# Delta rule steps of a two-block transformer kernel: inverse as three factors, 16-blocks solved on VectorE, two parts of neighbouring steps interleaved

## The chip, the cores and the metric

The kernel runs on one core of a Trainium2 chip, all in 32-bit floats, with batch 1 and 256 tokens. The metric is the device time of one execution in microseconds (us), lower is better. The engines are named as in the profile: PE (TensorE), DVE (VectorE), ACT (ScalarE), POOL (GpSimd) and SP (SyncE, which issues most transfers).

## What is computed

The program computes two transformer blocks. The first has dilated attention, a convolution branch, attention to a memory, and a mixture of 32 experts. The second works on 256 latent tokens and 256 context tokens: a state-space mixer (SSD), a gated delta rule (GDN) with 8 heads of 128, both in two directions and with the context's final state as the latents' first one, then a feed-forward layer. The change is in the gated delta rule. The reference solves a unit lower triangular system per chunk and head:

```python
def gdn_chunk_scan(q, k, v, log_a, beta, s0):
    ...
    a_mat = jnp.einsum("bclhd,bcshd->bclsh", k, k) * beta[:, :, :, None] * masked_exp(diff, strict)
    lhs = jnp.moveaxis(a_mat, -1, 2) + jnp.eye(CHUNK, dtype=a_mat.dtype)
    rhs = jnp.concatenate([v * beta[..., None], k * (beta * jnp.exp(g))[..., None]], -1)
    sol = lax.linalg.triangular_solve(lhs, jnp.moveaxis(rhs, 3, 2), left_side=True,
                                      lower=True, unit_diagonal=True)
    ...
    def step(s, inp):
        u_c, w_c, qk_c, qg_c, kd_c, dec_c = inp
        v_new = u_c - jnp.einsum("bhlk,bhkv->bhlv", w_c, s)
        o = jnp.einsum("bhlk,bhkv->bhlv", qg_c, s) + jnp.einsum("bhls,bhsv->bhlv", qk_c, v_new)
        s = s * dec_c[..., None, None] + jnp.einsum("bhlk,bhlv->bhkv", kd_c, v_new)
        return s, o
```

## The kernel before

The kernel takes chunks of 128 tokens, so each direction has four steps: two over the context, two over the latents. The table `STEPS` puts them in the order m = 0 to 7, directions alternating, so that step m needs the state of step m - 2. Steps 0 to 3 (context) are woven between the phases of the 32 experts by `mixed_schedule`, which gives each phase a cost and spreads the context phases over the expert phases in proportion; all engines follow that one list. Steps 4 to 7 (latents, `LATENT`) follow the SSD stage, after the experts, with parts of the modulation rows (`mod_part`, `mod_sum`, of a weight tile `ad4` to `ad11`) put between their phases.

Weights stream from HBM through a ring of six slots of 1 MB. SP issues a transfer when the piece that held the slot has been used by PE (`wait_freed`). In the experts stage each half of gate and up and each down product takes two slots.

PE writes into six banks of PSUM in turn (`MAIN`): `open_tile` waits until the tile six places earlier has been drained by ACT or DVE. One tile holds four heads, so each quantity of a step has two tiles, h = 0 and 1. `("gKK", m, h)` is the tile of that name.

Within a step the functions `gdn_pe`, `gdn_act`, `gdn_dve` and `gdn_pool` walk the same phases. "rows" transposes the keys and makes the rows of summed log decays (a matmul of a broadcast column with a triangular mask); "gram" makes K K^T, which DVE multiplies with beta and decay into the strictly triangular matrix A. Its inverse is formed in whole: the blocks of 16 on the diagonal by a product of powers (P2, X2, X4, X8), and then three levels of merging (32, 64, 128), each with a transpose (XT), a product (T) and another (Y), masks by POOL between them. "w" and "v" then apply it to the scaled keys and values, and "S" makes output (go2) and new state (gS). No phase of step m + 1 begins before the last of step m.

The recorded durations of an f32 matmul stand in two rows of the trace, and those of a transpose in one.

## Time and profile before

| | |
|---|---|
| median of 3 runs | 1868.62 us (1863.86 to 1870.5) |
| the profiled execution | 1869.31 us |
| its span | 1867.6 us, granted clock 0.956 |
| PE busy | 1708.2 us (91%) |
| DVE, ACT, POOL busy | 684.6 (37%), 435.7 (23%), 213.2 us (11%) |
| HBM read | 369.98 MB, 199 GB/s over the span |
| experts stage | about 440 to 1040 us |
| second block up to the delta steps | 1040 to 1293 us |
| delta steps 4 to 7 | 1293 to 1531 us |
| projection, feed-forward | 1531 to 1868 us |

Busy is the time in which an engine executes something that counts; waits aren't in it. The span is that of the profiled execution on the chip, a little shorter than its time, which the clock of the runs measures. A stage's bound is read from its own window, not from the share over the whole span.

### The profile page before, as it was taken

How to read it: one execution, taken by the hardware profiler on the slowest of the kernel's cores; microseconds unless marked ns; L12 is line 12 of the kernel's file. 1: busy time of each engine (PE TensorE's matmuls, PEld its weight loads, DVE VectorE, ACT ScalarE, POOL GpSimd, SP SyncE). 2: the span in 40 equal slices, each digit the busy share in tenths (PEclk: the TensorE clock that was granted, in tenths of full speed). 3: DMA queues.
4: the chain of work that ended last, by engine and by line, in shares of the span. 5: the costliest groups of instructions: out<-in, count | busy, mean ns of one | idle time of the engine just before them, and what ended most of it. 6: DMA issues, size and time to landing. Idle time of an engine off the chain costs nothing.

```text
span 1867.6 us, 25449 instructions
## 1 busy us (share of the span) xinstructions
PE 1708.2 (91%) x10656; PEld 1209.9 (65%) x10656; DVE 684.6 (37%) x1404; ACT 435.7 (23%) x889; POOL 213.2 (11%) x190
## 2 busy tenths in 40 slices
PE   7999999999888879999999899899989989699996
PEld 3558555456666547767766588666978874488842
DVE  2107113335434353323233377665355450400003
ACT  1010454013111123323332231322333430000000
POOL 2000000020000012221212100011342320100000
PEclk9999999998988889999999899999999999799998
DMA  7444335723999888979989434224121222244340
GB/s 242 163 148 143 128 125 190 251 103 135 372 394 350 326 317 343 416 318 365 415 340 393 171 137 148 90 91 176 62 91 46 91 91 90 90 138 178 123 155 38
DMA packets 124295, 372.69 MB, mean 200 GB/s; under 512 B 10523, under 2 KB 26517, under 8 KB 107413
## 3 DMA queue, kind: packets, MB, share of 16 engines
q1 hardware_dynamic: 118245, 361.12, 51.6%
q0 software_dynamic: 1568, 8.39, 1.2%
q10 hardware_dynamic: 4368, 1.54, 0.4%
q8 instruction: 87, 1.43, 0.3%
q14 instruction: 27, 0.22, 0.0%
HBM read 369.98 MB, written 1.05 MB: 199 GB/s over the span
## 4 chain that ended last, share of the span: by engine, by line
PE 77%; DMA 13%; DVE 7%; ACT 1%; issue 1%; SPq 0%; DVEq 0%; ACTq 0%
PE psum L1976 49%; PE psum L571 10%; DMA ring<-in_w_down 4%; PE psum L1775 4%; DMA ring<-in_w_up 4%; DMA ring<-in_w_in 4%; PE psum L1970 3%; PE psum L1816 2%; PE psum L1759 2%; PE psum L1797 1%; PE psum L2093 1%; PE psum L768 1%; PE psum L2123 1%; PE psum L557 1%; DVE area L1180 1%
## 5 line engine op out<-in xcount | busy, mean ns | idle before, releaser
L1976 PE MATMUL psum<-area,ring 128*128 128x256 f32 x1984 | 457.7, 391 | 15.1 <-DMA ring<-in_w_in 14.1
L1976 PE MATMUL psum<-ring,area 128*128 128x512 f32 (+1 forms) x1040 | 452.5, 595 | 8.6 <-DMA ring<-in_w_proj_mem 2.4
L1976 PEld LDWEIGHTS psum<-area,ring 128*128 128x128 f32 x1984 | 386.1, 197 | 75.2 <-DMA ring<-in_w_in 18.1
L1976 PEld LDWEIGHTS psum<-ring,area 128*128 128x128 f32 x1040 | 198.9, 193 | 252.7 <-issue 251.7
L571 PEld LDWEIGHTS psum<-area 128*128 128x128 f32 x2304 | 269.7, 194 | 34.7 <-issue 19.1
L571 PE MATMUL psum<-area 128*128 128x128 f32 x2304 | 281.0, 280 | 10.6 <-DVE area L1180 10.4
L949 ACT ACTIVATE area<-psum 128x512 f32<-128x512 f32 x236 | 138.7, 597 | 243.7 <-PE psum L571 127.8
L2249 ACT ACTIVATE area<-psum 128x512 f32<-128x512 f32 x116 | 66.4, 599 | 460.9 <-PE psum L1976 362.2
L1970 PE MATMUL psum<-const,area 128*128 128x128 f32 x736 | 120.6, 294 | 52.0 <-DVE area L1490 14.8
L1970 PEld LDWEIGHTS psum<-const,area 128*128 128x128 f32 x736 | 90.5, 149 | 97.4 <-issue 23.0
L1775 PE MATMUL psum<-ring,area 128*32 128x256 f32 x2048 | 124.8, 388 | 12.5 <-DMA ring<-in_w_up 12.3
L1775 PEld LDWEIGHTS psum<-ring,area 128*32 128x32 f32 x2048 | 64.0, 111 | 59.3 <-issue 24.0
L1144 DVE SCALAR_TENSOR_TENSOR area<-area,cols 128x268 f32<-128x268 f32 (+1 forms) x186 | 91.6, 492 | 6.6
L1797 PE MATMUL psum<-ring,area 128*32 128x256 f32 x1024 | 68.2, 398 | 19.8 <-DMA ring<-in_w_down 19.4
L1535 POOL TENSOR_TENSOR area<-area,const 128x512 f32<-128x512 f32 x48 | 60.1, 1274 | 219.2 <-PE psum L571 219.2
L913 ACT COPY area<-psum 128x256 f32<-128x256 f32 x62 | 23.1, 373 | 210.6 <-PE psum L1976 210.6
L1142 DVE TENSOR_SCALAR area<-area,cols 128x268 f32<-128x268 f32 (+1 forms) x62 | 22.1, 356 | 120.3 <-ACT area L913 119.1
L1514 POOL TENSOR_TENSOR area<-area 128x1024 f32<-128x1024 f32 x4 | 10.8, 2728 | 461.9 <-DVE area L2371 461.9
L1797 PEld LDWEIGHTS psum<-ring,area 128*32 128x32 f32 x1024 | 31.0, 113 | 50.0 <-DMA ring<-in_w_down 22.0
L1501 DVE TENSOR_TENSOR area<-psum,area 128x512 f32<-128x512 f32 x11 | 7.6, 691 | 151.5 <-PE psum L1976 151.5
L1232 DVE TENSOR_TENSOR area<-area,psum 128x512 f32<-128x512 f32 x48 | 32.9, 687 | 67.2 <-PE psum L571 67.1
L1222 DVE TENSOR_TENSOR area<-psum,area 128x512 f32<-128x512 f32 x48 | 33.2, 691 | 60.7 <-PE psum L571 60.2
(304 smaller groups left out, 1346.5 us busy)
## 6 DMA issues: line engine op xcount, KB each, us to landing
ring<-in_w_gate SPq DMA_DIRECT2D x64, 1024.0 KB, 9.6
ring<-in_w_up SPq DMA_DIRECT2D x64, 1024.0 KB, 11.5
ring<-in_w_down SPq DMA_DIRECT2D x64, 1024.0 KB, 11.3
ring<-in_w_in SPq DMA_DIRECT2D x29, 2048.0 KB, 8.4
ring<-in_w_ada SPq DMA_DIRECT2D x12, 2048.0 KB, 8.1
ring<-in_w_in SPq DMA_DIRECT2D x13, 1024.0 KB, 7.5
ring<-in_w_out SPq DMA_DIRECT2D x6, 2048.0 KB, 8.5
ring<-in_w_ffn_gate SPq DMA_DIRECT2D x5, 2048.0 KB, 7.8
```

Source lines behind the costliest of these rows:

```text
L571: last = nc.tensor.matmul(dst[:, i * P:(i + 1) * P], lhs(i), rhs(i), start=True, stop=True)
L949: nc.scalar.activation(dst, src, ACT.Copy, scale=scale).then_inc(drain_of(key), 1)
L1144: link(v.scalar_tensor_tensor(dst, src, w, dst, ALU.mult, ALU.add))
L1222: v.tensor_tensor(bb[h][7], four(key), bb[h][7], ALU.add).then_inc(drain_of(key), 1)
L1535: g.tensor_tensor(b[6], b[3], by_row(LEVELS[lev]), ALU.mult).then_inc(s["level_ready"], 1)
L1759: last = nc.tensor.matmul(dst[:, j * P:(j + 1) * P], h2[:, t, k * P:(k + 1) * P], place[:, t, q * P:(q + 1) * P], start=t == 0, stop=t == ...
L1775: last = nc.tensor.matmul(wide.dst[CAP * j:CAP * (j + 1), 0:2 * P], hcT[:, q % 2, k, rows], both[:, :, k % 4, j * P:(j + 1) * P], start=k ...
L1797: last = nc.tensor.matmul(dst[CAP * g:CAP * (g + 1), 0:256], actT_e[:, e % 2, CAP * j:CAP * (j + 1)], w[:, j % 2, g * 256:(g + 1) * 256], ...
L1816: nc.tensor.matmul(dst, placeT[:, q, t * P:(t + 1) * P], y_quad[:, q % 2, half * WIDE:(half + 1) * WIDE], start=True, stop=True).then_inc( ...
L1970: last = nc.tensor.transpose(t[0:width, j * P:j * P + rows], src, ident[0:rows, 0:rows])
L1976: last = nc.tensor.matmul(dst, lhs(k), rhs(k), start=first and k == 0, stop=final and k == count - 1)
L2249: nc.scalar.activation(dst, src, func).then_inc(drain_of(key), 1)
```

## The change

The step no longer forms the inverse in whole. A is split into its diagonal blocks of 16 and the rest. The blocks' inverse X comes from a recurrence over 15 columns on DVE, for all 64 blocks and heads at once: A's blocks are gathered to rows of 16, spread with a unit pattern to 2048 columns, PE sums them over each block with the mask `blk16` in four matmuls of 512 columns (gRep), so that each partition has its block's whole 16x16 matrix; then come 15 pairs of a product and a subtraction, each waiting for the one before, and eight writes into XT. With M = A_off X and M2 = M M, the inverse is applied to the right-hand side as factors (M2 is used twice, in gT and gw, and again in gx, and M once, in gv) rather than formed. What it is applied to is U = v beta less the scaled K S (gK), so the keys need no inverse of their own. The rows of summed decays are made by transposing a broadcast column of `cum`; the SSD stage's rows too. POOL no longer masks levels.

`delta_phases` puts the part of step m + 1 that needs no state (rows, gram, rep) between the phases of step m (kS, M, u, M2, t, w, x, v, out); the costs of the schedule between the experts follow that. The modulation tiles, the q sums and the normalized y of the SSD have new places in it. Per step PE's products of all heads go down to 14 from 23 in the latents.

```diff
+def delta_phases(steps):
+
+    order = [(phase, steps[0]) for phase in ("rows", "gram", "rep")]
+    for m in steps:
+        for phase in ("kS", "M", "rows", "u", "M2", "gram", "t", "w", "rep", "x", "v", "out"):
+            if phase not in ("rows", "gram", "rep"):
+                order.append((phase, m))
+            elif m + 1 in steps:
+                order.append((phase, m + 1))
+    return order
...
+    delta = {"rows": 2.4, "gram": 2.0, "rep": 3.6, "kS": 1.9, "M": 3.8, "u": 1.9, "M2": 1.9, "t": 1.9, "w": 1.9, "x": 1.9,
+             "v": 1.9, "out": 1.9}
...
+        MOD_PHASES = ["gram 4", "rep 4", "kS 4", "v 4", "v 5", "v 6", "u 7", "w 7", "v 7"]
...
+                        transposes(("gR", m, h), [cum[side][:, d, t, 16 + head:17 + head].to_broadcast([P, P])
+                                                  for head in range(4 * h, 4 * h + 4)])
...
+                if phase == "rep":
+                    pe.wait_ge(s["spread_ready"], m + 1)
+                    columns = b["spread"].rearrange("p i h j -> p (i h j)")
+                    for q in range(4):
+                        nc.tensor.matmul(open_tile(("gRep", m, q)), blk16, columns[:, 512 * q:512 * q + 512],
+                                         start=True, stop=True).then_inc(filled, 1)
+                if phase == "kS" and ci:
+                    for h in range(2):
+                        wait_drained(pe, ("gS", m - 2, h))
+                        eight("gK", h, of("kT"), lambda head: state[:, head, :])
+                if phase == "M":
+                    pe.wait_ge(s["XT_ready"], m + 1)
+                    for h in range(2):
+                        pe.wait_ge(s["off_ready"], 2 * m + h + 1)
+                        eight("gM", h, of("XT"), of("A"))
+                        eight("gMT", h, of("A"), of("XT"))
...
+                if phase == "v":
+                    for h in range(2):
+                        wait_drained(pe, ("gx", m, h))
+                        eight("gv", h, of("MT"), of("U"))
...
+                    for q in range(4):
+                        part = slice(32 * q, 32 * q + 32)
+                        ins = v.tensor_copy(b["pairs"][part, :, :], b["A"][part, :, part])
...
+                if phase == "rep":
+                    rep, Y, tmp = b["rep"], b["Y"], b["step"]
+                    link(v.tensor_copy(Y, unit_16.unsqueeze(2).to_broadcast([P, 16, GDN_HEADS])))
+                    for q in range(4):
+                        wait_drained(eng, ("gRep", m, q))
+                    for j in (range(15), range(15, 0, -1))[d]:
+                        left = (slice(j + 1, 16), slice(0, j))[d]
+                        n = left.stop - left.start
+                        link(v.tensor_tensor(tmp[:, 0:n, :], rep[:, left, :, j], Y[:, j:j + 1, :].to_broadcast([P, n, GDN_HEADS]), ALU.mult))
+                        link(v.tensor_tensor(Y[:, left, :], Y[:, left, :], tmp[:, 0:n, :], ALU.subtract))
+                    for head in range(GDN_HEADS):
+                        ins = v.tensor_tensor(b["XT"][:, head, :].rearrange("p (g j) -> p g j", j=16),
+                                              Y[:, :, head].unsqueeze(1).to_broadcast([P, 8, 16]),
+                                              blk16.rearrange("p (g j) -> p g j", j=16), ALU.mult)
+                    ins.then_inc(s["XT_ready"], 1)
...
-                        last = nc.tensor.matmul(dst[:, j * P:(j + 1) * P],
-                                                log_a[1][:, c - 2, d, 4 * q + j:4 * q + j + 1].to_broadcast([P, P]),
-                                                (upto, since)[d], start=True, stop=True)
+                        last = nc.tensor.transpose(dst[:, j * P:(j + 1) * P],
+                                                   cum[1][:, d, c - 2, 4 * q + j:4 * q + j + 1].to_broadcast([P, P]), ident)
```

Three places of the programs show what moved. The first is PE in the latent steps. Before, step m = 7: L1970 are transposes, L571 the products of all heads (8 to a pass), L2123 and L785 the modulation's part and sum.

```order
L1970 MATMUL psum<-const,area 128x128 x8
L571 MATMUL psum<-const,area 128x128 x8
L571 MATMUL psum<-area 128x128 x16
L2123 MATMUL psum<-ring,area 32x512 x8
L1970 MATMUL psum<-const,area 128x128 x8
L785 MATMUL psum<-area 128x512
L571 MATMUL psum<-area 128x128 x64
L2123 MATMUL psum<-ring,area 32x512 x8
L1970 MATMUL psum<-const,area 128x128 x8
L571 MATMUL psum<-area 128x128 x16
L1970 MATMUL psum<-const,area 128x128 x8
L571 MATMUL psum<-area 128x128 x8
```

Changed, from the modulation's sum in phase v of step 4 on (L771 and L2069 sum and part, L591 the products, L1916 transposes, L614 gRep, L778 the q sums):

```order
L771 MATMUL psum<-area 128x512
L2069 MATMUL psum<-ring,area 32x512 x8
L591 MATMUL psum<-area 128x128 x40
L1916 MATMUL psum<-const,area 128x128 x16
L591 MATMUL psum<-area 128x128 x16
L778 MATMUL psum<-const,area 128x1 x8
L591 MATMUL psum<-area 128x128 x40
L614 MATMUL psum<-area,const 128x512 x4
L591 MATMUL psum<-area 128x128 x16
L771 MATMUL psum<-area 128x512
L2069 MATMUL psum<-ring,area 32x512 x8
```

The first 40 products are go2 and gS of step 4, then gK, gM and gMT of step 5; the transposes are already step 6's keys and rows. Between gRep of step 6 and gv of step 5 stands gx alone (the 16 behind L614 are gx and gv).

The second place is DVE in a latent step. Before, step m = 6, from the rows (L1190) over the product with beta (L1203) to the additions of X2, X4 and X8 (L1222):

```order
L1190 TENSOR_SCALAR area<-psum,area 128x128 x16
L1203 SCALAR_TENSOR_TENSOR area<-psum,area 128x128 x8
L1180 SCALAR_TENSOR_TENSOR area<-area,const 128x512 x2
L1212 TENSOR_TENSOR area<-psum,area 128x512 x2
L1180 SCALAR_TENSOR_TENSOR area<-area,const 128x512 x2
L1382 SCALAR_TENSOR_TENSOR area<-psum,area 128x512
L1222 TENSOR_TENSOR area<-psum,area 128x512 x6
```

Changed, step m = 5 (the recurrence goes on in pairs of L1205 and L1206, down to 8 elements, 30 in all):

```order
L1177 SCALAR_TENSOR_TENSOR area<-psum,area 128x128 x8
L1184 COPY area<-area 32x256 x4
L1186 TENSOR_SCALAR area<-area,stats 128x128
L1187 SCALAR_TENSOR_TENSOR area<-area,stats 128x128
L1191 TENSOR_TENSOR area<-area,stats 128x2048
L1196 TENSOR_TENSOR area<-psum,area 128x512 x2
L1219 TENSOR_TENSOR area<-area,psum 128x512 x2
L1222 TENSOR_TENSOR area<-psum,area 128x512 x2
L1199 COPY area<-stats 128x128
L1205 TENSOR_TENSOR area<-area 128x120
L1206 TENSOR_TENSOR area<-area 128x120
```

Between the products with beta and the next work on U stand the copies, the spread of 2048 elements and the chain of small operations; gw and go1 (L1219, L1222) stand ahead of that chain and gx behind it.

The third place is PE between the experts. L1775 (changed: L1721) is a half of gate and up, L1797 (L1743) a down product, L571 (L591) delta products, L1970 (L1916) transposes. Before, in the middle of the experts stage:

```order
L1775 MATMUL psum<-ring,area 32x256 x32
L571 MATMUL psum<-area 128x128 x16
L1797 MATMUL psum<-ring,area 32x256 x16
L571 MATMUL psum<-area 128x128 x8
L1970 MATMUL psum<-const,area 128x128 x9
L1775 MATMUL psum<-ring,area 32x256 x16
L571 MATMUL psum<-area 128x128 x8
L1775 MATMUL psum<-ring,area 32x256 x16
L571 MATMUL psum<-area 128x128 x8
L1970 MATMUL psum<-const,area 128x128 x8
L1797 MATMUL psum<-ring,area 32x256 x16
L571 MATMUL psum<-area 128x128 x8
```

Changed, from the last product before step 2's gRep on (L614):

```order
L1721 MATMUL psum<-ring,area 32x256 x32
L591 MATMUL psum<-area 128x128 x8
L1743 MATMUL psum<-ring,area 32x256 x16
L614 MATMUL psum<-area,const 128x512 x4
L1916 MATMUL psum<-const,area 128x128
L1721 MATMUL psum<-ring,area 32x256 x16
L591 MATMUL psum<-area 128x128 x8
L1721 MATMUL psum<-ring,area 32x256 x16
L591 MATMUL psum<-area 128x128 x8
L1743 MATMUL psum<-ring,area 32x256 x16
L591 MATMUL psum<-area 128x128 x8
```

Before, a pass of eight stands between every two expert phases; now there are fewer, and gRep is followed by a gate half, gx, the next half, gv.

## Rows read from the trace of the kernel before

**Rows 1.** Windows by stage: start:end length, busy us (rows), granted clock, DMA share, GB/s.

```profile
440.00:767.00 327.00, 282.07 (x2525) 198.59 (x2524) 131.67 (x290) 78.09 (x200) 23.45 (x16) 0.91 0.88 342
...
767.00:1040.00 273.00, 252.43 (x2724) 188.15 (x2722) 90.32 (x181) 85.22 (x170) 57.84 (x46) 0.98 0.93 372
...
1293.00:1531.00 238.00, 218.38 (x1799) 195.84 (x1797) 119.79 (x234) 90.64 (x151) 87.43 (x73) 0.97 0.25 90
```

**Rows 2.** Windows of 20 us, same columns, beside the context delta steps.

```profile
740.00:760.00 20.00, 19.76 (x238) 15.06 (x234) 4.74 (x9) 8.13 (x18) 8.63 (x8) 1.00 1.02 419
...
800.00:820.00 20.00, 18.45 (x227) 14.74 (x225) 5.30 (x10) 5.83 (x12) 2.51 (x2) 1.00 0.62 249
```

**Rows 3.** Timeline of PE, SSD stage and its end: start, length, line, operation, tiles.

```profile
1228.40 13.97 PE L1976 MATMUL psum<-ring,area 128*128 128x512 f32 x32
...
1247.95 3.74 PE L752 MATMUL psum<-const,area 128*128 128x128 f32 x32
...
1293.53 1.04 PE L1970 MATMUL psum<-const,area 128*128 128x128 f32 x8
```

**Rows 4.** Timeline of delta step m = 6, all engines, with idle time and releaser.

```profile
1416.11 3.74 PE L571 MATMUL psum<-area 128*128 128x128 f32 x32
...
1419.77 1.93 PE L2123 MATMUL psum<-ring,area 128*32 128x512 f32 x16
...
1421.58 2.15 DVE L1203 SCALAR_TENSOR_TENSOR area<-psum,area 128x128 f32<-128x128 f32 x8
...
1424.28 1.02 PE L785 MATMUL psum<-area 128*128 128x512 f32 x2
...
1428.37 16.26 PE L571 MATMUL psum<-area 128*128 128x128 f32 x128 [3.07 <-DVE area L1180]
...
1451.20 0.69 DVE L1232 TENSOR_TENSOR area<-area,psum 128x512 f32<-128x512 f32 x1 [0.20 <-PE psum L571]
...
1451.94 0.66 PE L1970 MATMUL psum<-const,area 128*128 128x128 f32 x4 [0.24 <-DVE area L1232]
...
1452.64 0.60 ACT L949 ACTIVATE area<-psum 128x512 f32<-128x512 f32 x1 [0.30 <-PE psum L1970]
```

**Rows 5.** Timeline of DVE in the routing, small linked operations.

```profile
423.89 0.17 DVE L2638 TENSOR_TENSOR area<-area 128x16 f32<-128x16 f32 x1
...
424.10 0.17 DVE L2639 TENSOR_TENSOR area<-area,r_prio 128x16 f32<-128x16 f32 x1
```

**Rows 6.** Timeline of step m = 7, DVE beside POOL.

```profile
1505.95 2.50 POOL L1535 TENSOR_TENSOR area<-area,const 128x512 f32<-128x512 f32 x2 [2.23 <-PE psum L571]
...
1506.09 2.38 DVE L1418 TENSOR_TENSOR area<-area 128x8 f32<-128x8 f32 x2
```

**Rows 7.** Groups by form: count, busy us and mean ns, idle before.

```profile
L1222 DVE TENSOR_TENSOR area<-psum,area 128x512 f32<-128x512 f32 x48 | 33.2, 691 | 60.7 <-PE psum L571 60.2
...
L938 ACT ACTIVATE area<-area 128x128 f32<-128x128 f32 x32 | 9.3, 293 | 0.0
```

**Rows 8.** Timeline of DVE between steps m = 4 and m = 5.

```profile
1351.18 1.21 DVE L1390 TENSOR_TENSOR area<-area 128x1024 f32<-128x1024 f32 x1
...
1356.70 1.22 DVE L1405 TENSOR_TENSOR area<-area 128x1024 f32<-128x1024 f32 x1
...
1357.84 4.22 DVE L1190 TENSOR_SCALAR area<-psum,area 128x128 f32<-128x128 f32 x16
```

**Rows 9.** Timeline, first product of step m = 5, and end of m = 7.

```profile
1368.74 3.50 PE L571 MATMUL psum<-area 128*128 128x128 f32 x29 [1.73 <-DVE area L1180]
...
1530.22 0.69 DVE L1250 TENSOR_TENSOR area<-psum,area 128x512 f32<-128x512 f32 x1
```

**Rows 10.** Timeline of PE between the experts.

```profile
759.13 1.93 PE L1775 MATMUL psum<-ring,area 128*32 128x256 f32 x32
...
767.31 2.24 PE L1797 MATMUL psum<-ring,area 128*32 128x256 f32 x32
```

**Rows 11.** Windows of 2 us of PE behind a wait, with the granted clock.

```profile
1430.00:1432.00 2.00, 2.00 (x11) 0.52 0.00 0
```

686 lines of the change are left out of this document (288 added, 398 removed).

## The prediction

> **What bounds the kernel now.** I read the windows by stage first, to see which engine is full where the delta steps run. In 767 to 1040 us PE is busy 252.4 of 273 us and the DMA share is 0.93; in 1293 to 1531 us PE is busy 218.4 of 238, DMA 0.25, DVE 119.8 [rows 1]. So the last four delta steps (m = 4 to 7) are bound by PE alone, and the first four (m = 0 to 3), which lie between the experts, by PE and the weight stream together: one 20 us slice there moves 419 GB/s, another only 249 [rows 2]. The reader is to see that the stream has a ceiling, and falls under it where PE holds the ring. The timeline then gives prices. A matmul of two 128x128 f32 operands stands as two rows, so 32 rows in 3.74 us are 16 matmuls [rows 4], 0.228 us each; eight of them (all heads, one "pass") cost 1.83 us. Eight transposes are eight rows and take 0.94 us in a run, 1.04 with their tail; a matmul 512 wide is 13.97 / 16 = 0.87 us [rows 3]. A hand-over costs about 0.1 us from DVE to PE, and 0.25 from PE to ACT or DVE: 1451.89 to 1451.94, and four transposes later 1452.64 [rows 4].
>
> **The change on PE.** By the code a latent step before has 23 passes and five groups of transposes: 42.1 + 4.7 = 46.8 us. After: gKK, gQK, gK, gM, gMT, gu, gM2, gT, gw, go1, gx, gv, go2 and gS, 14 passes (25.6), two groups of transposes (1.9) and four matmuls of 512 columns for gRep (3.5): 31.0 us. The modulation parts (1.9) with their sums (0.9) [rows 4] stay, eight of each. If PE alone counted, four steps would give back over 60 us. A context step goes from 37.6 (m = 0, 1) or 41.3 (2, 3) to 23.7 or 25.5: 157.8 to 98.4, so 59 us less.
>
> **What it adds on DVE.** Per step four copies of 32x256, two small operations, one operation of 2048 elements, and the recurrence: 30 operations of 120 down to 8 elements, each waiting for the one before, 1,920 elements in all; then eight of 128. The trace has no such run, but linked operations of 16 elements start 0.205 us apart [rows 5], and 1024 elements take 1.22 us [rows 8]. From these two, an element costs about 1 ns and the rest of an operation 0.19: 30 x 0.19 + 1.9 = 7.7 us. The bound below is 30 x 0.17 + 1.9 = 7.0, the link free. The bound above is beside POOL: two operations of 8 elements took 2.38 us while POOL ran its pair of 2.50 [rows 6], so a POOL pair can hold DVE by its own length. Its mask for A starts when the spread is ready, 6 us ahead of the recurrence, and is over by then; I take 7.7. By the same prices the 2048 elements are 2.3, the eight XT writes 1.8, the copies 1.2, the small ones 0.5.
>
> **A latent step walked through**, from XT of step m ready on DVE to XT of step m + 1 ready. DVE adds the first half of gx of step m - 1 (0.7) and hands over (0.1); PE does gv, 1.8, or 3.7 at the half clock (why is below): 4.5 us. Then the modulation's sum and part, which stand ahead of the output, 2.8: 7.3. go2 and gS, 3.7: 11.0. gK of step m, 1.8: 12.8. gM and gMT, 3.7: 16.5. Transposes of keys and rows for m + 1, 1.9: 18.4. ACT's scaling (eight of 0.29) and DVE's subtraction end at 15.2, so gu doesn't wait: 20.2. gM2: 22.0. First half of gKK and hand-over, 1.2: 23.2, and from here DVE carries. Products with beta 2.15, copies 1.2, small 0.5, spread 2.3: 29.4. gQK's products and gw follow on DVE; PE meanwhile runs gT, gw and go1 until 32.0, since go1's bank is free only when gQK's product has left it. gRep 3.5: 35.5. ACT waits for all four tiles and copies, 0.25 + 4 x 0.60: 38.2. Recurrence 7.7 and XT 1.8: 47.7, say 48. PE has only gx after gRep, and then stands still for some 10 us. Durations of DVE and ACT are [rows 4, 7].
>
> Before, the period is 59.6 us (gP2 starts at 1368.74 and at 1428.37 [rows 4, 9]). Now the stage. Up to XT of 4 nothing covers: DVE is through its 16 + 8 operations at 8.4, copies and small 10.1, spread 12.4, gRep 16.0, ACT 18.5, recurrence and XT 28.0. To XT of 5 it is the step without its first 11 us, with the q sums (1.8) added, and DVE first has gated y and the q squares, 1351.18 to 1357.84 before [rows 8], which delay gu by 1.5: 40.3. To XT of 6, 48 + 1.8; to XT of 7, 48. The last part, without gS and without a next step, but with three modulation parts: 37. POOL's masks or k_rest beside DVE's copies, 1.5 in three steps: 4.5. Together 207.6, against 237.4 from 1293.53 to 1530.91 [rows 3, 9]: **-30 us**. Half of what PE saves is given to the chain through DVE.
>
> **SSD stage.** Its 16 matmuls of rows per step, 3.74 us, become 16 transposes, 1.9. PE runs there with hardly a gap from 1228 on [rows 3], and DVE's work lies under the gates' 13.97 us. Three steps of 1.8, the first waits for DVE anyway: **-5**.
>
> **Experts stage.** From 767 on the old order still holds 126 us of PE work of delta steps, the new one 91 (rows, gram and rep of step 0 lie ahead of expert 16 in its schedule): 252.4 - 35 = 217. PE now has a gate part (1.93), gx (1.83) and one more part or a down product (2.1) between gRep and gv [rows 10], 5.8 us, against 2.6 + 7.7 + 1.8 + 0.7 = 12.8 on ACT and DVE: 7 us of standing still in three steps, 4 in the first, 25 together. With some 12 of other waits 254, against a floor of the stream of 372 x 273 / 417 = 244: **-19**. Ahead of 767 the stream moved 342 GB/s over 327 us. The channels are thinner between the experts now (104 of 224 units, rather than of 273), so it should reach 365: 306, **-21**; the bounds are 0 and, at 417, 268 us.
>
> Edits that cost nothing: fewer masks on POOL at the start (hidden by the first projections), the normalized y put into step 7 (DVE idles there; 2.7 without that cover), two unit rows on DVE (0.5 without cover).
>
> **Sum.** 30 + 5 + 19 + 21 = 75. The profiled execution took 1869.3 us for a span of 1867.6, and the median of the runs is 1868.6: 1869.3 - 75 = **1794 us**.
>
> **The clock.** After a wait of PE for 3 us the granted clock is 0.52 in 1430 to 1432, near the 1.2 of the two levels 1.2 and 2.4 GHz [rows 11], and the run of 128 rows from 1428.37 took 16.26 us [rows 4], where 64 x 0.228 is 14.6. I charge 1.8 per step, on gv. The Trainium skill (TensorE: Matmul & The Clock Gate, "HAM oscillation — how this bites in real kernels") describes a kernel in which every round waited long enough for the next to start at the half clock. The trace agrees that a wait is followed by it, and the rule speaks against a change that puts 10 us of waiting into each step.
>
> **Rivals.**
> 1. The experts stage gives nothing: each recurrence holds DVE, an expert's product waits behind it, its transpose on PE waits for that, and the stream idles. For it: 12.8 us against 5.8 of cover. Against: PE has 35 us less to do after 767. 1869 - 35 = 1834. Chance 0.18.
> 2. The stream reaches its ceiling in most of the stage: 268 + 244 instead of 306 + 254 is 48 lower; with 60% of it 1765. For it: the slice of 419. Against: the gather (16 matmuls) and the scatter (four of 512) still take PE 7 us per four experts without using weights. Chance 0.12.
> 3. Slower than before, by one mechanism: PE keeps the half clock all through the delta steps, because passes of 1.8 us between waits never bring it back. PE has some 25 us on the path of each latent step: 4 x 25, less 7 charged already, and some 27 more in the context steps: 1794 + 120 = 1914. It decides from about 63% of that on. Against: the clock was back within 4 us of 1428. Chance 0.05. The skill's rule, applied to every step, is this rival.
> 4. POOL holds DVE: four POOL pairs a step, some 9 us in all, each on the path: 1794 + 8 x 9 = 1866, no change. For it the pair at 1506. Against: two of them lie under PE's passes. Chance 0.04.
> The forecast has 0.60 and its own range, 1778 to 1812; 0.01 goes to what I can't name. Some 0.3% (5.6 us) is what a measurement of this kernel can tell. Faster 0.91, within 0.3% 0.04, slower 0.05. The range of 1762 to 1838 takes in rivals 1 and 2 at their values.
>
> **What would show it.** Right: gRep 48 us apart in the latent steps; 30 rows of DVE per step some 0.26 us apart; PE idle for 10 us ahead of gv, released by DVE; granted clock low just behind it; the last latent output 458 us behind the experts' end rather than 493; that end near 998. Wrong: periods near 60 by POOL or the clock, or an experts stage as long as before with a lower DMA share.

## The result: 26 us faster, a third of what was forecast

The changed kernel takes 1840.59 us (median of 4 runs, 1837.36 to 1843.69) beside 1866.24 for the kernel before in the same comparison: a ratio of 0.986, 95% interval 0.9832 to 0.9888. The forecast was 1794, range 1762 to 1838: the direction was right, the size wrong, and the time lies just above the range. The profiled execution took 1839.77 us for a span of 1838.0, against 1869.31 before.

The stages first, as in [rows 1]: windows of the changed kernel, with start:end, length, busy us of PE, weight loads, DVE, ACT and POOL, granted clock, DMA share, GB/s.

```profile
440.00:740.00 300.00, 240.54 (x2051) 159.47 (x2052) 112.17 (x257) 59.10 (x166) 3.75 (x2) 0.88 0.88 341
767.00:1034.00 267.00, 226.16 (x2352) 156.77 (x2352) 120.30 (x318) 69.31 (x152) 22.76 (x20) 0.92 0.93 373
1289.00:1508.00 219.00, 159.04 (x1156) 127.78 (x1155) 154.66 (x394) 65.29 (x132) 40.38 (x34) 0.88 0.29 105
```

PE is busy in 159 of 219 us of the latent steps, where it was busy in 218 of 238 before. It was freed of 59 us, and the stage got 19 shorter in these windows. The marks of the timeline give it more exactly:

| from ... to | before | changed | forecast | measured |
|---|---|---|---|---|
| start of the second block's first products (experts, scatter, hand-over) | 1047.29 | 1043.32 | -40 | -4.0 |
| from there to the first delta transposes of step 4 | 246.2 | 245.9 | -5 | -0.4 |
| from there to the last latent output | 237.4 | 213.2 | -30 | -24.2 |

The last output ends at 1502.42 in the changed kernel and at 1530.91 in the kernel before [rows 9]; behind it the two differ by 1 us. The step that failed is the experts stage, 36 us short; the SSD stage is 4.6 us short of its forecast and the latents 5.8. Next, the timeline of the changed kernel (start, length, engine, line, tiles, idle time and releaser), the places that the walk of a latent step names; L614 is gRep, L591 the products of the heads, L771 and L2069 the modulation's sum and part, L1205, L1206 and L1208 the recurrence and the writes into XT:

```profile
1043.32 5.40 PE L1922 MATMUL psum<-area 128*64 128x256 f32 x16 [0.99 <-ACT area L2195]
...
1289.20 1.92 PE L1916 MATMUL psum<-const,area 128*128 128x128 f32 x16
...
1301.45 6.09 PE L614 MATMUL psum<-area,const 128*128 128x512 f32 x8 [4.91 <-DVE area L1191]
...
1320.40 0.68 DVE L1364 SCALAR_TENSOR_TENSOR area<-psum,area 128x512 f32<-128x512 f32 x1
...
1321.22 2.05 PE L771 MATMUL psum<-area 128*128 128x512 f32 x2 [8.98 <-DVE area L1364]
...
1323.20 3.64 PE L2069 MATMUL psum<-ring,area 128*32 128x512 f32 x16
...
1347.74 3.60 PE L614 MATMUL psum<-area,const 128*128 128x512 f32 x8
...
1396.72 2.05 PE L591 MATMUL psum<-area 128*128 128x128 f32 x16 [2.28 <-DVE area L1196]
...
1398.61 3.60 PE L614 MATMUL psum<-area,const 128*128 128x512 f32 x8
...
1402.25 2.05 ACT L952 COPY area<-psum 128x512 f32<-128x512 f32 x4 [9.02 <-PE psum L614]
...
1404.43 0.35 DVE L1205 TENSOR_TENSOR area<-area 128x120 f32<-128x120 f32 x1 [4.64 <-ACT area L952]
...
1412.52 0.17 DVE L1206 TENSOR_TENSOR area<-area 128x8 f32<-128x8 f32 x1
...
1412.72 2.40 DVE L1208 TENSOR_TENSOR area<-area,const 128x128 f32<-128x128 f32 x8
...
1415.77 3.56 PE L591 MATMUL psum<-area 128*128 128x128 f32 x16 [11.78 <-DVE area L1219]
...
1439.76 2.55 DVE L1184 COPY area<-area 32x256 f32<-32x256 f32 x4
...
1447.89 3.60 PE L614 MATMUL psum<-area,const 128*128 128x512 f32 x8
...
1508.29 1.97 PE L1916 MATMUL psum<-const,area 128*128 128x128 f32 x8 [5.72 <-DVE area L1436]
```

The reader sees the predicted shape: gRep, ACT's copies, 30 linked DVE operations from 1404.43 to 1412.69, eight writes, and PE standing still for 11.78 us ahead of gv. gRep starts at 1301.45, 1347.74, 1398.61 and 1447.89: 46.3, 50.9 and 49.3 us apart, where 40.3, 49.8 and 48 were forecast, with 4.5 for POOL over the three as a sum of its own.

One caution for all that follows. The experts stage differs between executions of one kernel: a variant further down that leaves it alone (QK first) began the second block at 1053.37 in its profiled run, which was its slowest of four (1833.24 to 1846.39). A difference of 5 us there means little in one trace; one of 15 does, and so do the differences between the medians.

### The profile page after: what moved, and what is told of

The parts are those of the page before. It is cut to its first block, busy times and chain, and to the rows that moved or that the text cites. A ratio compares the mean times of both kernels' runs of the same rounds, so it can differ in the third digit from the quotient of the medians.

```text
span 1838.0 us, 22881 instructions
## 1 busy us (share of the span) xinstructions
PE 1595.0 (87%) x9344; PEld 1076.6 (59%) x9344; DVE 741.9 (40%) x1707; ACT 382.0 (21%) x830; POOL 113.0 (6%) x111
## 4 chain that ended last, share of the span: by engine, by line
PE 72%; DMA 13%; DVE 10%; ACT 2%; issue 2%; SPq 0%; DVEq 0%; ACTq 0%
PE psum L1922 49%; PE psum L591 7%; DMA ring<-in_w_up 5%; DMA ring<-in_w_in 4%; PE psum L1721 4%; DMA ring<-in_w_down 3%; PE psum L1916 2%; DVE area L1205 2%; PE psum L614 1%; PE psum L1762 1%; PE psum L1743 1%; DVE area L1206 1%; PE psum L1705 1%; PE psum L2069 1%; DVE area L1208 1%
## 5 line engine op out<-in xcount | busy, mean ns | idle before, releaser
L591 PE MATMUL psum<-area 128*128 128x128 f32 x1536 | 196.2, 287 | 61.4 <-DVE area L1219 56.1
L591 PEld LDWEIGHTS psum<-area 128*128 128x128 f32 x1536 | 186.5, 200 | 84.7 <-DVE area L1219 58.3
L1721 PE MATMUL psum<-ring,area 128*32 128x256 f32 x2048 | 137.0, 416 | 34.6 <-DMA ring<-in_w_up 34.6
L2195 ACT ACTIVATE area<-psum 128x512 f32<-128x512 f32 x116 | 66.4, 599 | 457.7 <-PE psum L1922 360.2
L1916 PE MATMUL psum<-const,area 128*128 128x128 f32 (+1 forms) x544 | 89.2, 295 | 44.9 <-DVE area L1467 14.8
L1721 PEld LDWEIGHTS psum<-ring,area 128*32 128x32 f32 x2048 | 68.9, 118 | 90.4 <-issue 60.6
L1916 PEld LDWEIGHTS psum<-const,area 128*128 128x128 f32 (+1 forms) x544 | 69.9, 151 | 78.6 <-issue 20.1
L1743 PE MATMUL psum<-ring,area 128*32 128x256 f32 x1024 | 68.5, 401 | 16.6 <-DMA ring<-in_w_down 16.4
L1478 DVE TENSOR_TENSOR area<-psum,area 128x512 f32<-128x512 f32 x11 | 7.6, 692 | 151.1 <-PE psum L1922 151.1
L932 ACT COPY area<-psum 128x512 f32<-128x512 f32 x96 | 54.4, 589 | 52.4 <-PE psum L591 38.7
L1743 PEld LDWEIGHTS psum<-ring,area 128*32 128x32 f32 x1024 | 31.1, 114 | 46.5 <-DMA ring<-in_w_down 19.0
L1441 DVE TENSOR_TENSOR area<-psum,area 128x512 f32<-128x512 f32 x8 | 5.5, 692 | 128.4 <-PE psum L1922 128.4
L1205 DVE TENSOR_TENSOR area<-area 128x120 f32<-128x120 f32 (+14 forms) x120 | 31.2, 260 | 48.8 <-ACT area L952 45.0
L1872 DVE TENSOR_TENSOR area<-psum,area 128x128 f32<-128x128 f32 x32 | 9.3, 290 | 96.1 <-ACT area L1824 96.0
L1219 DVE TENSOR_TENSOR area<-area,psum 128x512 f32<-128x512 f32 x48 | 32.1, 686 | 26.7 <-PE psum L591 26.4
```

Of the source, the lines that this page charges most:

```text
L591: last = nc.tensor.matmul(dst[:, i * P:(i + 1) * P], lhs(4 * h + i), rhs(4 * h + i), start=True, stop=True)
L932: nc.scalar.copy(b[name][:, 4 * h:4 * h + 4, :], src).then_inc(drain_of((key, m, h)), 1)
L1205: link(v.tensor_tensor(tmp[:, 0:n, :], rep[:, left, :, j], Y[:, j:j + 1, :].to_broadcast([P, n, GDN_HEADS]), ALU.mult))
L1219: v.tensor_tensor(b["U"][:, heads, :], b["U"][:, heads, :], four(key, h), sign).then_inc(drain_of((key, m, h)), 1)
L1721: last = nc.tensor.matmul(wide.dst[CAP * j:CAP * (j + 1), 0:2 * P], hcT[:, q % 2, k, rows], both[:, :, k % 4, j * P:(j + 1) * P], start=k ...
L1743: last = nc.tensor.matmul(dst[CAP * g:CAP * (g + 1), 0:256], actT_e[:, e % 2, CAP * j:CAP * (j + 1)], w[:, j % 2, g * 256:(g + 1) * 256], ...
```

## Experiments

Two theories on the experts stage. A: the delta steps' recurrences hold DVE, DVE's additions of gx and the experts' products queue behind them, PE waits, and that takes back what PE saves. B: the stage is set by the stream, the experts and the channels, whatever a delta step costs. In the latents the question was the chain of a step. The kernel before ran beside each group of experiments, with medians from 1866.4 to 1870.2; ratios are to it.

### The delta steps of the context moved behind the experts

```diff
-                order.append(("context", name))
+                delta = " " in name
+                (late if delta else order).append(("context", name))
...
-    return order + [("context", phase) for phase, _ in context[taken:]]
+    return order + late + [("context", phase) for phase, _ in context[taken:]]
```

> The changed kernel with the delta phases of steps 0 to 3 taken out from between the experts and done right behind them, in the same order; channels and experts keep their places. In the changed kernel the experts end at about 1034 us, as in the kernel before (1038). Theory A (the delta steps, above all the recurrences on DVE, hold PE and so the weight stream): without them the experts end 25 to 40 us sooner, near 1000. Theory B (weight stream, experts and channels alone set the stage, delta work fits beside them): the end stays at 1025 to 1034. Either way the four steps then stand uncovered behind the experts, some 45 us each: the whole takes 1841 + 180 us under B, 1841 + 145 under A.

Measured: 1986.3 us (1982.5 to 1990.4), ratio 1.0624 (1.0588 to 1.066). With no delta step left among the experts, the last scatter still begins at 1003.35, 24.1 us ahead of the changed kernel (1027.44) and 29.3 ahead of the kernel before (1032.62). That is just under theory A's 25 to 40 us and far from B's end of 1025 to 1034; the total is A's 1841 + 145. My -40 could not be had even by removing these steps outright: from 740 to 980 us the stream now moves 413 GB/s, close to the 417 to 419 of its fastest slices. Between 440 and 740 us this stream, too, reads no more than 101.7 MB (339 GB/s over 300 us), against 102.3 in the changed kernel.

### One column of the recurrence instead of fifteen

```diff
-                    for j in (range(15), range(15, 0, -1))[d]:
+                    for j in (range(1), range(15, 14, -1))[d]:
```

It leaves out 14 of 15 columns, so the blocks' inverse is incomplete.

> The changed kernel with only one of the recurrence's 15 columns (28 of 30 linked DVE operations per step left out, so the inverse of the blocks is left incomplete). They take about 7 us a step. Latent steps: XT of step 4 and the periods to 5, 6 and 7 are each 7 us shorter, 28 in all, if the recurrence is wholly on their path, as my walk through a step has it. Experts stage: theory A, 15 to 28 us shorter too (total near 1790); theory B, unchanged within 4 us (total near 1812).

Measured: 1789.46 us, ratio 0.9577 (0.9551 to 0.9603), 51 less than the changed kernel. The second block begins at 1028.07 (-15.3) and the stretch from step 4's gRep to the transposes behind the delta steps is 173.4 instead of 206.8 us (-33.4). The second is the chain: 28 had been forecast for it, and the four steps gave 10.3, 7.3, 7.4 and 8.4. The first is the experts stage's part. The waits of PE between 740 and 1030 us in the changed kernel (engine, line, released by: us in total, times, longest) name the place:

```profile
PE psum L591 <- DVE area L1219: 20.7, 3, 8.1
...
PE psum L1916 <- DVE area L1872: 7.2, 1, 7.2
```

gv waits for gx's additions, which queue behind a recurrence, and once an expert's transpose waits for its product (L1872) in the same way. In the run with one column the first row is

```profile
PE psum L591 <- DVE area L1219: 1.1, 2, 0.5
```

So theory A holds for some 15 us, and not for the rest of what was missing.

### Neighbouring steps not overlapped

```diff
-        for phase in ("kS", "M", "rows", "u", "M2", "gram", "t", "w", "rep", "x", "v", "out"):
...
+    phases = ("rows", "gram", "rep", "kS", "M", "u", "M2", "t", "w", "x", "v", "out")
+    return [(phase, m) for m in steps for phase in phases]
```

> The changed kernel with its phases in plain order (rows, gram, rep, kS, M, u, M2, t, w, x, v, out of a step, then the next step), so that nothing of neighbouring steps overlaps. By my walk a latent step would be 28 us to XT and some 32 behind it, 60 instead of 51: three periods, +27 in all from the overlap lost. Theory A: the experts stage grows too, by 10 us or more, since PE stands still for longer; theory B: it doesn't.

Measured: 1876.05 us, ratio 1.0047 (1.0027 to 1.0068). The factored inverse alone, one step after the other, is no faster than the kernel before, though PE has 40.3 us of work in a latent step of 58.3. The overlap is worth 35 us by the medians; in the profiled executions 16.1 up to the start of the second block (1059.41) and 23.2 from there to the transposes behind the delta steps (27 forecast). The 16 us are theory A's again, which asked for 10 or more.

### The recurrence dealt out in pieces

gx stands ahead of gRep, and DVE does 4 columns at rep, 6 at v, the rest and the XT writes at out.

> The changed kernel with gx ahead of gRep and the recurrence cut in pieces on DVE: 4 columns, then the subtraction of gv, 6 columns, the output's additions, the rest. If PE's standing still (11.8 us ahead of gv in steps 5 to 7) is only the order on DVE, the period falls from 51 to about 45: 15 to 18 us less in the latents. If DVE's own work (about 36 us a step) and the hand-overs bound it, less than 8. Theory A: the experts stage gains as well, 10 us or so; theory B: nothing there.

Measured: 1831.28 us, ratio 0.9801 (0.9766 to 0.9836). The second block begins at 1035.52 (-7.8), while gRep in the latents stays 48.0, 50.05 and 48.9 us apart, 146.9 in all against 146.4, where 15 to 18 less or less than 8 had been forecast: gv's wait of 11.78 us is gone, but gM now waits 8.9 us, for XT. I read the latent step from this as a cycle from XT over M, rows, gram and gRep to the next XT; the wait that was taken away lay beside it and gave nothing.

### gram and rep earlier

```diff
-        for phase in ("kS", "M", "rows", "u", "M2", "gram", "t", "w", "rep", "x", "v", "out"):
+        for phase in ("kS", "M", "rows", "gram", "u", "M2", "rep", "t", "w", "x", "v", "out"):
```

> Edit: in the list of phases, gram and rep of step m + 1 stand right behind rows and M2 of step m (kS, M, rows, gram, u, M2, rep, t, w, x, v, out), and the recurrence's 15 columns are dealt out on DVE: 3 at rep, 3 at t, 2 at w, 3 at x, the rest and the XT writes at v. Theory A (the latent period of 50 us is a chain from XT over M, rows, gram, gRep to the next XT, in which w, go1, x, v and out of the old step are only queued in between): from XT, M 3.7, rows to spread 13.6, gRep and its copies 5.7, then 10.7 of recurrence and XT writes with 5.2 of additions between them and about 1 of waits: period 40 to 41, three times 9 less than the changed kernel's 50, the stage 27 to 30 us shorter, and in the experts stage 8 to 12 us less, as expert products wait for a few columns only: about 1802 us. Rival B (PE's and DVE's sums bound the period at about 50 whatever the order, as after the earlier spreading of columns, which left gRep 50.05 us apart): period 48 to 50, about 1830 us.

> Edit: only gram of step m + 1 moves ahead of u and M2 of step m; rep, recurrence and the rest stay where the changed kernel has them. Theory A (up to gRep the latent step is carried by PE's queue, in which 1.6 to 2.3 us are waits for the bank of gQK, drained late by DVE): those waits and the 0.5 ahead of gT go, DVE is ready earlier without use; gRep 47.5 to 48 us apart instead of 50, the stage 6 to 8 us shorter, about 1833 us. Rival B (DVE's rows, products and spread carry it, gKK's place decides): the whole 3.7 us per step come back, three periods of 46.3, the stage 11 us shorter, about 1829.

Measured: both moves with the columns dealt out 1820.42 us, ratio 0.9746 (0.9723 to 0.9768), but gRep 46.7, 50.9 and 46.2 us apart, not 40. gram alone, ahead of u, 1863.69 us, ratio 0.9975 (0.9961 to 0.9989): 23 us slower than the changed kernel, where both theories had it faster, with periods of 54.9, 61.3 and 55.6. The trace of that run, timeline, with L778 the q sums and L1196 gQK's product with its mask:

```profile
1391.98 4.88 DVE L1184 COPY area<-area 32x256 f32<-32x256 f32 x4
...
1397.60 2.29 DVE L1191 TENSOR_TENSOR area<-area,stats 128x2048 f32<-128x2048 f32 x1
1399.81 1.28 DVE L1196 TENSOR_TENSOR area<-psum,area 128x512 f32<-128x512 f32 x2
...
1400.64 3.54 PE L778 MATMUL psum<-const,area 128*128 128x1 f32 x16 [7.49 <-DVE area L1196]
1404.04 8.52 PE L591 MATMUL psum<-area 128*128 128x128 f32 x48
```

and its windows there:

```profile
1400.00:1404.00 4.00, 3.36 (x16) 3.39 (x17) 1.09 (x2) 0.00 (x0) 2.46 (x2) 0.50 0.00 0
1404.00:1412.00 8.00, 8.00 (x46) 8.00 (x47) 1.84 (x4) 1.17 (x2) 0.00 (x0) 0.62 0.00 0
```

Six tiles behind gQK stands the q sums' tile (in the next step gT's). It needs gQK's bank, which DVE drains only behind copies and spread, so PE waits 7.49 us, and then runs at a clock of 0.50 and 0.62: 24 matmuls (48 rows) take 8.52 us, where the same phases take 5.67 at full clock in the fastest kernel below. The moved phase did not lengthen the chain; it moved the tile that needs the late bank ahead of what used to cover it. The run with rep early has the same wait (7.49 at 1377.45).

### gQK's product first, and the banks free early

In DVE's phase "gram" the loop moves ahead of the copies of A's blocks:

```diff
+                    for h, heads in halves if side else ():
+                        key, part = ("gQK", m, h), b["QK"][m % 2][:, heads, :]
+                        eng.wait_ge(s["gdn_maskedT"], 2 * (m - 4) + h + 1)
+                        v.tensor_tensor(part, four("gQK", h), part, ALU.mult).then_inc(drain_of(key), 1)
                     for q in range(4):
                         part = slice(32 * q, 32 * q + 32)
                         ins = v.tensor_copy(b["pairs"][part, :, :], b["A"][part, :, part])
```

> Edit: DVE multiplies gQK's products (1.28 us) ahead of its copies, small operations and spread, instead of behind them; the order of phases is the changed kernel's. Theory A: each latent step of the changed kernel has PE waiting 1.6 to 2.3 us behind gw's first half for the bank of gQK, and then gRep is ready to go; with the bank free, gRep comes as early as the spread allows, now 1.3 later: 1 to 1.5 us less per step, three periods, 3 to 5 us in all, about 1836. Rival B (DVE's chain alone sets gRep): 1.3 us more per step, about 1844.

> Edit: the order kS, M, rows, gram, u, M2, t, w, rep, x, v, out; gQK's products ahead of the copies on DVE; the 15 columns dealt out 4 at rep, 4 at x, the rest and the XT writes at v. Theory A (in the two runs with gram ahead of u the gain was eaten because PE's tiles rotate through six banks: gT, or the q sums, needed the bank that gQK had, and waited 6.0 to 7.5 us until DVE had done copies and spread; with that gone the chain from M to M is 40 to 42 us): gRep 40 to 43 us apart in the latent steps against 46.2 to 50.9, the stage 15 to 20 us shorter than in the run with gram and rep early, about 1803 us. Rival B (DVE's own sum of work, with its additions among the columns, is the bound near 46): periods 45 to 47, about 1815.

Measured: the first, this edit alone, 1839.45 us (1833.24 to 1846.39), ratio 0.983 (0.9788 to 0.9871). Its total can't tell 3 us; its latent stretch is 203.6 instead of 206.8 us, as theory A had it. The second, with the order kS, M, rows, gram, u, M2, t, w, rep, x, v, out and the columns at rep, x and v: 1802.8 us (1799.28 to 1806.38), ratio 0.9643 (0.9613 to 0.9673), 38 less than the changed kernel, at the forecast 1803. Its timeline, gRep and, in the second period, the q sums (L778):

```profile
1291.56 5.50 PE L614 MATMUL psum<-area,const 128*128 128x512 f32 x8 [6.09 <-DVE area L1211]
...
1335.82 3.60 PE L614 MATMUL psum<-area,const 128*128 128x512 f32 x8
...
1369.91 1.84 PE L778 MATMUL psum<-const,area 128*128 128x1 f32 x16
...
1377.96 3.60 PE L614 MATMUL psum<-area,const 128*128 128x512 f32 x8
...
1418.87 3.60 PE L614 MATMUL psum<-area,const 128*128 128x512 f32 x8
```

Periods of 44.3, 42.1 and 40.9; the latent stretch is 181.2 us (-25.6), the second block begins at 1032.24 (-11.1). The q sums no longer wait. The run joins three edits (order, gQK first, columns dealt out), so the 38 us are not the banks' alone: gQK first by itself took 3.2 us from the stretch, and the columns dealt out by themselves left the periods as they were. No run takes one of the three out of this kernel.

### The first latent period

```diff
-        MOD_PHASES = ["gram 4", "rep 4", "kS 4", "v 4", "v 5", "v 6", "u 7", "w 7", "v 7"]
+        MOD_PHASES = ["gram 4", "rep 4", "x 4", "v 4", "v 5", "v 6", "u 7", "w 7", "v 7"]
```

> Edit: of the modulation's nine places in the list of phases the third moves from 'kS 4' to 'x 4', into PE's wait ahead of gv; nothing else. Theory A: the first latent period was 46.3 us (1301.45 to 1347.74) and not my 40.3 because PE, with XT of step 4 ready at 1320.9, first did a modulation sum that waited for DVE (gated y and squares stood ahead of DVE's part of it) and a part, 1321.22 to 1326.84, ahead of gM. The first period falls to 40 to 41, the kernel by 5 to 6 us, to about 1835. Rival B (DVE's gated y and squares, 5.5 us, delay M and u anyway): less than 2 us.

Measured: 1841.35 us, ratio 0.9851 (0.981 to 0.9892): no difference from the changed kernel. The first period did fall, from 46.3 to 42.9, but the second rose from 50.9 to 54.0. Windows of this run at gv of step 4 and at gw of step 5:

```profile
1361.00:1368.00 7.00, 6.48 (x26) 4.24 (x30) 3.73 (x6) 0.00 (x0) 0.00 (x0) 0.53 0.00 0
...
1394.00:1398.40 4.40, 3.55 (x17) 3.55 (x18) 3.28 (x6) 0.00 (x0) 2.50 (x2) 0.61 0.00 0
```

and of the changed kernel at the same two places:

```profile
1364.90:1371.00 6.10, 6.10 (x35) 3.90 (x35) 2.62 (x4) 0.00 (x0) 0.00 (x0) 0.77 0.00 0
...
1396.00:1398.60 2.60, 1.88 (x16) 1.88 (x17) 2.60 (x6) 0.00 (x0) 2.46 (x2) 1.00 0.00 0
```

The same instructions take 7.6 instead of 6.0 us (gv, sum and part, to 1369.08) and 3.5 instead of 1.9 (gw's second half with go1) at the lower clock, 3.1 us together, which is what the second period lost. The first period had given back a part before: gM, now first behind a wait of 8.29 us, takes 6.77 us instead of 3.84. What made the clock fall at gw of step 5 and not in the changed kernel, the runs do not show.

### What holds the stream ahead of 740 us

```diff
-                    lambda k: hB[0][:, k, :], KD).then_inc(filled, 1)
+                    lambda k: hB[0][:, k, :], KD // 2).then_inc(filled, 1)
```

for the channels' products; for the taps, `for tap_i in (0, TAPS - 1) if side == 0`. Both leave part of the sums out. The run "context late" moves all context work but the first four channels and the decays behind the experts.

> Edit: all of the context work but the first four channels and the decays is moved behind the experts, where nothing covers it; this prices what bounds the experts stage and is no better kernel. With the delta steps alone moved, the stream had still read only 101.8 MB from 440 to 740 us, as much as every other kernel, and the last scatter began at 1003. Theory A (ahead of 740 it is the context's channels and SSD states, with their hand-overs, that hold the stream, so that a cheaper delta step had nothing to give there): 108 MB or more by 740, the last scatter at about 980 to 990 (214.6 MB at 417 GB/s take 515 us from 440, and a gather and scatter of 7 us for each of eight groups lets it dip). Rival B (the experts' own order of transfers holds it, gathers and scatters above all): again 102 to 103 MB by 740, scatter at 1000 to 1003. The total is that of a kernel with some 250 to 300 us of context work laid bare, about 2100 to 2180.

> Edit: PE's products of the context channels (3.6 us each, two in a row between the experts) run over half of their 8 input tiles, so over half the sum; all transfers stay. Theory A (ahead of 740 the stream is held by PE's own context passes: PE stands in one queue, and 5.4 + 3.6 us of channels between experts keep it from freeing the ring): 23 times 1.8 us of PE less, 106 to 110 MB by 740 instead of 102.3, the last scatter 10 to 20 us earlier, about 1825. Rival B (it is DVE's convolution and the hand-overs to turned channels): 102 to 103 MB by 740, less than 5 us.

> Edit: DVE's convolution of the context channels takes 2 of its 5 taps (so the channels are wrong sums), about 1.5 us less of DVE for each of 26 channels; PE unchanged. Theory A (PE's passes hold the stream): 102 to 103 MB by 740, less than 5 us. Rival B (DVE holds it): 105 MB or more by 740, 8 us or more.

Measured: context late 2024.51 us, ratio 1.0835 (1.0805 to 1.0865); half channels 1821.36, 0.9733 (0.9706 to 0.976); two taps 1842.99, 0.9859 (0.9831 to 0.9886). The window 440 to 740 us, kernel before:

```profile
440.00:740.00 300.00, 255.72 (x2216) 178.49 (x2218) 125.26 (x278) 69.21 (x181) 14.40 (x8) 0.90 0.87 335
```

All later context work moved out:

```profile
440.00:740.00 300.00, 196.00 (x2126) 105.18 (x2118) 46.81 (x112) 39.99 (x102) 0.00 (x0) 0.82 0.98 402
```

Half the channels' products:

```profile
440.00:740.00 300.00, 214.53 (x1978) 128.59 (x1974) 119.55 (x278) 63.88 (x173) 8.23 (x6) 0.88 0.93 368
```

Two taps:

```profile
440.00:740.00 300.00, 236.51 (x2040) 156.17 (x2039) 74.73 (x175) 57.39 (x162) 3.75 (x2) 0.89 0.88 342
```

Taking 37 us from DVE changes nothing (342 GB/s against 341); taking 26 us of PE's channel products gives 27 GB/s and starts the second block at 1023.50, 19.8 us earlier. Theory A had forecast both. With the context work gone the stream runs at 406 to 418 GB/s in every slice of 20 us from 460 to 740; the last scatter begins at 929.40, well ahead of the 980 to 990 forecast, and the total is below the 2100 to 2180. So ahead of 740 PE's channels in PE's one queue hold the stream: halving them gives back 27 of the 61 GB/s between 341 and 402. The rest of the gap was not split further.

### Everything together, and one part of it

The kernel of 1802.8 us, with the modulation part at x 4, POOL's masks for k_rest at x, and its two gate products at M 7 and u 7; then with the k_rest masks alone.

> Edit: the kernel of the run before in this call, and besides the modulation part at 'x 4', POOL's masks for k_rest moved from M2 to x, and its two gate products from u 5 and u 6 to M 7 and u 7. Theory A (DVE's four copies of 32x256 take 1.18 us alone and 2.4 to 4.9 beside POOL's long operations; they stand on the chain to gRep): copies 1.2 us in every step, 1.2 to 3.7 us less per step, and 4 to 6 for the part: 8 to 12 us less than that run, about 1793 us. Rival B (the copies' length is not POOL's doing, or the time is lost elsewhere beside POOL): only the part's 4 to 6 us, about 1798.

> Edit: the kernel of 1802.8 us with POOL's masks for k_rest moved from M2 to x, nothing else. Theory A (in the run with all edits together the copies came down to 1.17 us each time, but the modulation part gave its gain back, and POOL's two gate products in step 7 with the part cost 5.2 us there): the first three copies' groups come down from 2.0, 3.7 and 2.2, the last step stays at 53.9, 2 to 4 us less, about 1800. Rival B (k_rest beside the first columns of the recurrence costs DVE what it saved at the copies): no change, 1802 to 1804.

Measured: 1804.06 us, ratio 0.9648 (0.9617 to 0.9679), and 1802.63 us, 0.9638 (0.9615 to 0.9662): neither beats the 1802.8. POOL is the cause of the long copies. With POOL's work moved away from them:

```profile
1367.00 1.17 DVE L1204 COPY area<-area 32x256 f32<-32x256 f32 x4
```

and in the run with gram and rep early, where POOL runs 4.5 us beside them:

```profile
1368.78 4.89 DVE L1200 COPY area<-area 32x256 f32<-32x256 f32 x4
```

But with all edits the last step, from gRep of step 7 to the transposes behind the steps, takes 59.1 instead of 53.9 us, which eats the gain. With k_rest alone it takes 53.7 and the latent stretch 179.7 instead of 181.2. The trace of the run with all edits shows where most of the 5.2 us go: into the eight XT writes of step 7, beside POOL's two gate products (L1594), which had been moved there.

```profile
1432.38 8.05 DVE L1161 TENSOR_TENSOR area<-area,const 128x128 f32<-128x128 f32 x8
...
1435.25 4.73 POOL L1594 TENSOR_TENSOR area<-area,gdn_gain 128x1024 f32<-128x1024 f32 x2
```

In the kernel of 1802.8 us the same writes take 3.88 us, and the products behind them wait 1.29 us instead of 4.69.

### The rows of the SSD stage by matmuls again

> Edit: the SSD stage's rows of summed decays by 16 matmuls per step again instead of 16 transposes; nothing else. My prediction gave that part of the change 5 us. Theory A (the traces: from the second block's first product to the first delta transposes before 246.2 us, changed 245.9; PE waits there for DVE's decay products, the time saved goes into that wait): 0 to 1 us slower, 1840 to 1842. Rival B (PE's 1.8 per step count, something else hid them in the change): 5 us slower, about 1845.

Measured: 1839.52 us, ratio 0.9848 (0.9819 to 0.9878), no difference from the changed kernel. From the second block's first products to gRep of step 4 it takes 259.5 instead of 258.1 us: the edit is worth 1.4, not 5. PE waits for DVE's decay products there in either, 6.56 us here and 8.40 in the changed kernel at the first of them.

## Why the prediction was right or wrong

**Latents, -30 against -24.2: right in mechanism, the size a fifth too large.** The walked step was right in its order of waits. Its sum was 203.1 us and 4.5 for POOL; the stage took 213.2. The second and third period, 50.9 and 49.3, are 1.1 and 1.3 us over the walk without POOL's term. The recurrence took 8.26 us instead of 7.7 (the sum written down, 30 x 0.19 + 1.9, gives 7.6): 0.35 and 0.28 us for 120 elements against 0.17 for 8, so 1.3 ns an element on average, where I took 1. The XT writes took 2.4 instead of 1.8. The copies took 2.52 and 2.55 instead of 1.2 in these two periods, which is the POOL term (1.5 charged for each); so other rows of the walk were some 1.4 us too long.

The first period, 46.3 instead of 40.3, holds two things that I left out. gRep of step 4 comes behind a wait of PE of 4.91 us and takes 6.09 us instead of 3.6, at a granted clock of 0.60 from 1301.4 to 1307.6; I had charged the clock on gv alone. And at kS 4 a modulation sum and a part stand ahead of gM on PE, 1321.22 to 1326.84, at a clock of 0.50, with XT of step 4 written by 1320.5. Moving them gave 3.4 us in that period and showed, too, that the clock took most of the gain elsewhere. The last part, from gRep of step 7 to the last output, took 54.5 instead of 52.6.

**SSD, -5 against -0.4.** A PE edit costed at its length, in a stage in which I had noted that one of the waits hides it. The wait for DVE hides nearly all: 1.4 us by the run with the old rows.

**Experts behind 767, -19 against nothing that a trace can tell.** The stretch of 767 to 1034 has PE busy for 226 us, 9 more than I took, at a clock of 0.92 instead of 0.98, and not busy for 41, where I had 37. The standing still behind recurrences that I costed at 25 us is there (20.7 and 7.2). What failed is the step from PE's sum to the stage's length: in the kernel before 20.6 us of PE's idle time were enough for the stream to end at the same place. From 740 to 980 us PE is busy 28 us less than before, and the stream moves 371 GB/s instead of 372. Windows of the kernel before:

```profile
740.00:980.00 240.00, 225.82 (x2504) 172.44 (x2497) 77.72 (x160) 79.95 (x158) 53.26 (x42) 0.99 0.92 372
```

and of the changed one, with two slices:

```profile
740.00:980.00 240.00, 197.76 (x2099) 136.14 (x2102) 118.64 (x335) 66.35 (x141) 25.20 (x22) 0.92 0.92 371
...
820.00:840.00 20.00, 11.95 (x101) 7.72 (x100) 12.60 (x44) 2.96 (x7) 0.00 (x0) 0.80 1.02 413
...
860.00:880.00 20.00, 19.50 (x247) 14.45 (x245) 10.37 (x28) 9.96 (x17) 2.98 (x3) 1.00 0.81 315
```

In the slice from 820 PE is busy 11.95 us of 20 and the stream is at 413 GB/s, its ceiling; in the one from 860 PE works nearly all the time and the stream falls to 315. My reading is that PE's saving falls into slices in which the ring is full of requests anyway, while each wait behind a recurrence delays the freeing of slots; the run with one column, 15 us earlier, bears out the second half; the first is argued from these slices and no run tests it alone. That PE has less to do is worth something only where PE was what held the stream.

**Experts ahead of 767, -21 against about -5.** The failed step in words of the prediction: the channels are thinner between the experts now, so the stream should reach 365 GB/s. It moved 341 instead of 335 to 740 us, 1.9 MB more, some 4.5 us at 417 GB/s; the runs that leave the channels as they are moved 337 to 344 there, so even the -5 is rough. The schedule's costs place context phases between expert phases by share; the channels' own passes on PE, two in a row, remain where they are long, and the run with half of them shows that these hold the stream.

**Rivals.** The outcome is rival 1 in its size (1834 forecast, 1840.6 measured) with its mechanism in part: recurrence, product and transpose in a queue are there, but they explain some 15 us of the missing 36, and the channels hold the stream where most of the rest was expected. Rival 2 (the ceiling) was wrong for the whole stage, right for single slices; only with the delta steps moved out did the stream come near it from 740 to 980 us, with 413 GB/s. Rival 3 was wrong as stated: the clock came back to 1.00 within each step (window 1371 to 1378), yet it is 0.932 over the span against 0.956 before. The Trainium skill's page TensorE: Matmul & The Clock Gate (section "HAM oscillation — how this bites in real kernels") is borne out in the small: gv behind the 11.78 us takes 3.4 to 3.8 us, as charged. Rival 4 was wrong in its price, right in that POOL lengthens DVE's copies.

**What was never weighed** was the order of the phases itself. The chain was taken as given, and the tile rotation appeared in the walk once, as "go1's bank is free only when gQK's product has left it". That wait, 1.0 to 2.3 us in the changed kernel, was the thread to a version 38 us faster.

## What to carry to other kernels

When a step is rewritten to do less on the full engine, work out first what the stage would take with that step gone altogether; a run with it moved out gave 29 us here where 40 had been summed. In a cycle over several engines look for the edge that closes it (here XT to M to gram to gRep to XT) and shorten that; shortening what lies beside it gave nothing here, and a long dependent run on one engine belongs in pieces between what others wait for. When phases are reordered over rotating banks, list which tile stands as many places behind each late-drained one: that is the next wait, and its length is that of whatever the drain queues behind.

## What the runs showed of the hardware

- DVE's copies of 32x256 from memory to memory take 0.29 us alone and up to 1.2 us beside POOL's operations of 128x512 and 128x1024 (four in 1.17 and 4.89 us); DVE's writes of 128x128 from memory to memory take 0.37 us alone and up to 2.42 beside POOL's products of 128x1024. Eight operations of 128x128 that read from PSUM kept their 2.15 to 2.16 us beside POOL (L1177 with L1583 and L1514).
- Linked DVE operations of 128x8 to 128x120 take 0.17 to 0.35 us and start 0.03 to 0.04 us behind the end of the one before, with no further wait.
- After a wait of PE of 7.49 us its next 12 us ran at a granted clock of 0.50 and 0.62; of a gain of 3.4 us in one place the clock took 3.1 back at two others.
